# A two-block transformer on one Trainium2 core: a layer norm moved into the merge loop, gate tiles emptied by another engine, bias rows stored in longer runs

## What is computed

```python
swa_bias, swa_mask = swa_bias_and_mask(positions, rel_bias)      # once: bias by distance, per head
for l in range(DEPTH):                                           # DEPTH = 2
    h = rms_norm(x, g_mix[l])
    q_a, k_a, v_a, u_b, cq_c, ckv_c, kpe_c, gate_logits = split(h @ w_in[l])
    y_a = swa_attention(q_a, k_a, v_a, sinks, swa_bias, swa_mask)   # window of 128
    y_b = conformer_conv(u_b, ...)        # GLU, causal depthwise conv of 31 taps, LayerNorm, swish
    y_c = mla_attention(cq_c, ckv_c, kpe_c, ...)                    # latent attention
    branches = einsum('bsnc,ncd->bsnd', stack([y_a, y_b, y_c]), w_branch[l])
    gates = sigmoid(gate_logits)                                 # 3 x 1024 columns
    x = x + einsum('bsnd,bsnd->bsd', gates, branches) @ w_out[l]
    x = x + square(relu(rms_norm(x, g_mlp[l]) @ w_up[l])) @ w_down[l]
```

## Time and profile before

| | us |
|---|---|
| median of 3 runs | 4863.44 (4861.99 to 4865.29) |
| the profiled execution, its own time | 4864.94 |
| span of its instructions | 4863.1 |

### The profile page before, as it was taken

The page is one execution under the profiler, slowest core; times in us unless marked ns, Lnnn a source line. Parts: engine busy times, 40 slices in busy tenths (PEclk is TensorE's granted clock), DMA queues, the critical chain, the costliest instruction groups (busy, mean ns, idle before and its releaser), DMA issues. The chain is left out here.

```text
span 4863.1 us, 70463 instructions
## 1 busy us (share of the span) xinstructions
PE 4100.0 (84%) x29198; PEld 3345.2 (69%) x29198; DVE 2234.5 (46%) x3547; ACT 1453.8 (30%) x2611; POOL 124.8 (3%) x97
## 2 busy tenths in 40 slices
PE   6888999988889999699948888799997656657998
PEld 5666777766667777567737777688886545545887
DVE  4575544436755443334564444433333444354434
ACT  3334432223344222324222222322223201433322
POOL 0111000001100000000000000000000000000000
PEclk8999999999989999879969999899998766777999
DMA  4331444423314443100100000121121001001322
GB/s 155 89 93 50 132 156 157 160 75 95 79 56 152 156 158 137 44 14 1 61 4 3 4 3 22 38 67 61 61 68 47 6 0 35 18 0 61 96 95 78
DMA packets 320251, 338.93 MB, mean 70 GB/s; under 512 B 25792, under 2 KB 298848, under 8 KB 313696
## 3 DMA queue, kind: packets, MB, share of 16 engines
q1 hardware_dynamic: 315520, 330.56, 21.2%
q10 hardware_dynamic: 4448, 4.36, 0.3%
HBM read 313.92 MB, written 20.97 MB: 69 GB/s over the span
## 5 line engine op out<-in xcount | busy, mean ns | idle before, releaser
L276 DVE TENSOR_TENSOR weights_lo<-weight_ring,weights_hi 128x1024 fp32r<-128x1024 f32 x370 | 453.4, 1225 | 1410.0 <-ACT weights_hi L272 1410.0
L272 ACT ACTIVATE weights_hi<-weight_ring 128x1024 fp32r<-128x1024 f32 x370 | 392.2, 1060 | 1633.0 <-PE banks L323 1554.3
L323 PE MATMUL banks<-mlp_x_lo,weights_hi 128*128 128x512 f32 (+1 forms) x1280 | 480.3, 375 | 0.0
L323 PE MATMUL banks<-mlp_hidden_hi,weights_hi 128*128 128x512 f32 (+1 forms) x1280 | 477.1, 373 | 0.0
L323 PE MATMUL banks<-mlp_hidden_lo,weights_hi 128*128 128x512 f32 (+1 forms) x1280 | 476.6, 372 | 0.0
L323 PE MATMUL banks<-mlp_hidden_hi,weights_lo 128*128 128x512 f32 (+1 forms) x1280 | 476.0, 372 | 0.0
L2568 PE MATMUL banks<-weight_ring 64*64 64x64 f32 x10368 | 341.2, 221 | 86.4 <-DVE weight_ring L2686 45.7
L2568 PEld LDWEIGHTS banks<-weight_ring 64*64 64x64 f32 x10368 | 320.5, 137 | 105.2 <-DVE weight_ring L2686 52.9
L323 PE MATMUL banks<-mlp_x_hi,weights_hi 128*128 128x512 f32 x768 | 308.1, 401 | 20.2 <-DVE mlp_x_lo L307 9.5
L323 PE MATMUL banks<-mlp_x_hi,weights_lo 128*128 128x512 f32 x768 | 305.4, 398 | 0.0
L323 PEld LDWEIGHTS banks<-mlp_hidden_hi,weights_hi 128*128 128x128 f32 x1280 | 240.8, 188 | 52.6 <-issue 6.7
(11 more groups left out here) (533 smaller groups left out, 7361.3 us busy)
## 6 DMA issues: line engine op xcount, KB each, us to landing
weight_ring<-in_w SPq DMA_DIRECT2D x64, 1024.0 KB, 5.5
mod_chunks<-in_mod_w SPq DMA_DIRECT2D x24, 2048.0 KB, 10.3
weight_ring<-in_w_in SPq DMA_DIRECT2D x41, 1024.0 KB, 5.2
weight_ring<-in_w_up SPq DMA_DIRECT2D x32, 1024.0 KB, 5.7
weight_ring<-in_w_down SPq DMA_DIRECT2D x32, 1024.0 KB, 5.1
weight_ring<-in_w_in SPq DMA_DIRECT2D x52, 512.0 KB, 3.8
weight_ring<-in_w_out SPq DMA_DIRECT2D x16, 1024.0 KB, 5.3
gate_logits_dram<-gates_staged SPq DMA_DIRECT2D x48, 256.0 KB, 3.5
```

The lines of the kernel that those rows point to most:

```text
L272: act.activation(self.w_hi[:, t % 2], self._raw(t), ACT.Copy).then_inc(self.w_rounded, 1)
L276: dve.tensor_tensor(self.w_lo[:, t % 2], self._raw(t), self.w_hi[:, t % 2].bitcast(F32), ALU.subtract)\
L323: mm = pe.matmul(bank, a[:, k, :], b[:, k, t0:t0 + w], start=(k == 0 and n == 0), stop=(k == KD - 1 and n == 2))
```

## The change

1. **Bias stores.** The four mask DMAs go. The table of a part now holds 16 rows of 257 elements, the 128 values between one mask value ahead and 128 behind, just as the rows lie in DRAM. One store is then 8 runs of 16,448 bytes. Such a table is twice as large, so there are 3 instead of 8: from part 3 on ACT waits, before it writes a table, for the four stores of the part that used it. POOL fills the mask values first.
2. **Gate tiles.** `evacuate` goes from ACT to DVE, where it multiplies by the norm's row straight from the bank. The POOL step and its semaphore `scaled` go. DVE's order is: evacuate tile n, then the rest of the weights of tile n+2. The seven copies of the positional keys go from group 3's place in POOL's list to the phase's beginning, where they wait only for `placed`.
3. **Norm in the merge.** The phase `conv_finish` goes. Its steps become a class `ConvNorm` whose parts are called inside the merge's loops, behind the work of units 0 to 12. The branches are merged in the order window, latent, convolution (`MERGE_ORDER`), and the first loads of the merge are issued in the merge.

```diff
-                sp.wait_ge(filled, 16 * BLOCKS)
                 for n in range(parts_out):
                     sp.wait_ge(taken, (n + 1) * chunks // parts_out)
+                    width = held * row_out if n < parts_out - 1 else (held - 1) * row_out + P + 1
                     for b in range(BLOCKS):
-                        src = bias[n][32 * b:32 * b + 8].rearrange("h (q k) -> h q k", k=P)
-                        sp.dma_start(rows_of(b, P // parts_out * n, P // parts_out), src).then_inc(stored, 16)
+                        sp.dma_start(rows_of(b, n, width), bias[n % len(bias)][32 * b:32 * b + 8, 0:width])\
+                            .then_inc(stored[n % len(bias)], 16)
...
-                pool.memset(masked[:, :], MASKED).then_inc(blank, 1)
+                for n in range(len(bias)):
+                    pool.memset(table(n)[:, :, 0:1], MASKED)
+                    pool.memset(table(n)[:, :, P + 1:], MASKED).then_inc(blank, 1)
...
-                act.wait_ge(blank, 1)
-                for b in range(BLOCKS):
-                    act.dma_start(bias_dram[b].rearrange("h q k -> q h k"), over(masked[:, :], SWA_HEADS))\
-                        .then_inc(filled, 16)
...
+                    n, at = c // 4, c % 4 * 4
+                    if at == 0 and n < len(bias):
+                        act.wait_ge(blank, n + 1)
+                    elif at == 0:
+                        act.wait_ge(stored[n % len(bias)], stores_of(n - len(bias)))
...
-    def evacuate(self, act, n):
-        act.wait_ge(self.summed, n + 1)
+    def evacuate(self, dve, n):
+        dve.wait_ge(self.summed, n + 1)
...
-        act.activation(out, self.banks[n % 2][rows, :], ACT.Copy).then_inc(self.emptied, 1)
+        dve.tensor_tensor(out, self.banks[n % 2][rows, :], self.row[rows, :], ALU.mult).then_inc(self.emptied, 1)
...
     def dve(self, dve, halves):
         for n in self.finished(halves):
+            self.evacuate(dve, n)
             self.rest(dve, n + 2)
...
+MERGE_ORDER = (0, 2, 1)
...
         def _(pe):
+            conv.averages(pe)
             for n in range(MERGE_UNITS):
...
+                if n == 5:
+                    conv.columns(pe)
+                if n == 9:
+                    conv.widen(pe)
```

More of the change, by code:

```diff
@@ L885, in _ @@
                     act.wait_ge(made, c + 1)
-                    own = chunks // parts_out
-                    act.activation(bias[c // own][:, c % own * BANK:(c % own + 1) * BANK], ps[:, c % 8, :], ACT.Copy)\
-                        .then_inc(taken, 1)
+                    n, at = c // 4, c % 4 * 4
[3 more added lines that the diff above has]
+                        act.wait_ge(stored[n % len(bias)], stores_of(n - len(bias)))
+                    act.activation(table(n)[:, at:at + 4, 1:P + 1], ps[:, c % 8, :].rearrange("p (q k) -> p q k", k=P),
+                                   ACT.Copy).then_inc(taken, 1)
                 act.wait_ge(reduced, 1)
@@ L971, in __init__ @@
         self.landed, self.stored = [sem(f"landed{s}") for s in range(2)], [sem(f"stored{s}") for s in range(3)]
-        self.rounded, self.ready, self.summed, self.emptied, self.scaled = (
-            sem(n) for n in ("rounded", "ready", "summed", "emptied", "scaled"))
+        self.rounded, self.ready, self.summed, self.emptied = (
+            sem(n) for n in ("rounded", "ready", "summed", "emptied"))
         part = 2 * KD * P
@@ L1133, in _ @@
                 closing(sp)
[L1135 to L1141, removed]
         @block.tensor
@@ L1266, in __init__ @@
         self.keys, self.gated = keys, gated
-        self.spread, self.timed, self.folded, self.placed, self.copied = (
-            kit.ph.sem(f"kpe_{s}") for s in ("spread", "timed", "folded", "placed", "copied"))
+        self.spread, self.timed, self.folded, self.placed = (
+            kit.ph.sem(f"kpe_{s}") for s in ("spread", "timed", "folded", "placed"))
     def sync(self, sp, u, adjusted):
@@ L1338, in _ @@
             pool.wait_ge(padded, 1)
-            gates.pool(pool, (0, 1))
+            beside.pool(pool)
         @block.tensor
@@ L1669, in logit @@
     def logit(self, sp, n):
-        sp.dma_start(self.slots[:, n % 3, :], self.logits[n]).then_inc(self.read[n % 3], 16)
+        sp.dma_start(self.slots[:, n % 3, :], self.logits[MERGE_ORDER[n // KD] * KD + n % KD]).then_inc(self.read[n % 3], 16)
     def __call__(self, sp):
@@ L1676, in __call__, with merge_branches @@
             self.logit(sp, n)
-def merge_branches(kit, ys, ys_hi, ys_lo, loads, merged, bent_slots, product, following):
+def merge_branches(kit, ys, ys_hi, ys_lo, loads, merged, bent_slots, product, conv, following):
     nc, ph, ps = kit.nc, kit.ph, kit.ps
@@ L1688, in merge_branches @@
         "w_rounded", "w_ready", "x_rounded", "x_cut", "x_ready", "summed", "bent", "timed", "added"))
-    xs = [(ys[s][:, k, :], ys_hi[s][:, k, :], ys_lo[s][:, k, :]) for s in range(3) for k in range(4)]
+    xs = [(ys[s][:, k, :], ys_hi[s][:, k, :], ys_lo[s][:, k, :]) for s in MERGE_ORDER for k in range(4)]
     def raw(n):
@@ L1696, in cut_in @@
         s, t = n // KD, n % KD
-        return [4 * (s + 1) + t - 1] if s < 2 and 1 <= t <= 4 else []
+        if s == 0:
+            return [4 + t - 1] if 1 <= t <= 4 else []
+        return {12: [8, 9], 13: [10, 11]}.get(n, [])
     with ph as block:
@@ L1701, in _ @@
         def _(sp):
+            loads(sp)
             sp.wait_ge(w_ready, 2)
@@ L1737, in round_x @@
             def round_x(i):
+                if i >= 8:
+                    act.wait_ge(conv.finished, i - 7)
                 act.activation(xs[i][2], xs[i][0], ACT.Copy).then_inc(x_rounded, 1)
@@ L1742, in keep_high @@
                 act.activation(xs[i][1], xs[i][0], ACT.Copy).then_inc(x_ready, 1)
-            weights(0)
             for i in range(4):
@@ L1749, in _ @@
             keep_high(3)
+            weights(0)
             weights(1)
```

180 lines of the change are left out of this document (87 added, 93 removed).

## The result

The changed kernel takes 4821.65 us in the median of four executions (4820.95 to 4823.27), the kernel before in the same session 4862.72. The ratio is 0.9914, with a 95% interval of 0.9903 to 0.9926: 41 us faster, where 74 were forecast, and 3.7 us above the upper end of the range. The profiled execution has a span of 4820.1 us, 43.0 less than before.

What follows compares the result with a forecast made beforehand. DVE's list was taken to bound much of the window attention, stores the opening, PE the merge. Bias stores -16, gate tiles -28 and norm -30 summed to -74, giving a median of 4790 us, range 4770 to 4818.

Steps and rivals of the forecast that it cites:

- a leftover of 1.5: Opening: 1.5 us of leftover stores standing in front of the next weights, to be taken off the gain of 16.6.
- 24 KB per engine and us: Opening: rate from input loads with long rows; with 8 engines a part's store takes 2.7 us, phase end 35.5.
- The bound at the slow end: Opening: at the old 82 GB/s the eight parts take 51 us and nothing is gained, 0 instead of -16.
- rival (a): Opening: stores stay slow, ACT waits for landings at 82 GB/s, opening ends where it did; 4806 us, chance 0.14.
- The share of 37.5%: Opening: old stores' mean share of 16 DMA engines, under a half, taken to show that a store uses 8 engines.
- the 14.9 us: Attention phases: PE's 6 waits for ACT's exponents, part of the possible 14.9 + 8.4 + 8.8 us; about 10 gained.
- the bound of -18: Gate tiles: fast end per layer instead of -14, if the window attention's clock, reading 0.90, stays up.
- The two waits of half a microsecond: Latent attention: two PE waits behind ACT's evacuation that the gate tiles' change removes, -1.0 us per layer.
- rival (e): Gate tiles: taps are slow for another reason than POOL, +5 instead of -10 per layer; 4820 us, chance 0.04.
- The cutting of the first branch: Merge: ACT and DVE cut the first branch's tiles in 5.2 us, to 472.4, while PE sums for the norm.
- Rival (d): Merge: it turns serial, each of the norm's 13 steps waiting for another engine; 4881 at 3.5 us a step, chance 0.03.

Runs made afterwards that it cites:

- e2: The changed kernel with the heads' table rows on every fourth partition, the same 32 stores of 8 long runs: 4783.45 us, ratio 0.9837.
- e3: The changed kernel with rows on every fourth partition and one store of 32 rows per part, 8 stores instead of 32: 4779.07 us, ratio 0.9828.
- e7: e3 with a POOL product of SBUF rows into an unread tile put back for each gate tile: 4797.3 us, ratio 0.9863.
- e8: e3 with three POOL fills for each gate tile, reading nothing from SBUF, of about the product's length: 4780.05 us, ratio 0.9828.
- e5: The kernel before with the gate tiles' change alone (DVE empties them, key copies moved): 4832.66 us, ratio 0.9937.
- e6: The kernel before with the norm of the convolution spread over the merge, nothing else: 4832.82 us, ratio 0.9938.
- e1: The changed kernel with the opening of the kernel before (mask DMAs, eight tables, stores in 512-byte runs): 4800.82 us, ratio 0.9867.
- e4: The changed kernel with the old opening (masks, 512-byte runs) and rows on every fourth partition: 4795.21 us, ratio 0.9855.
- e9: The changed kernel with the heads' table rows on every second partition, otherwise the same: 4794.59 us, ratio 0.9851.
- e10: e4 with one store of 32 rows per part, 512 runs of 512 bytes: 4788.73 us, ratio 0.9842.

## Why the prediction was wrong, point by point

**Bias stores: wrong in sign.** Forecast -16 (the prediction's own 16.6 less a leftover of 1.5 is 15), measured +23.7. The steps ahead of the stores held: first operand at 3.96 (4.3 forecast), first store at 16.9. The step that failed is the rate of a store, "24 KB per engine and us", taken from the input loads because the runs are long like theirs. With eight engines, which was right (49.6%), it was 8.9 KB, so that the 32 stores took 57 us where some 20 were priced. What the loads and the stores don't share is which rows they touch: the loads have 128 partitions, a store has 8 neighbours. e2 changed only that and got 3.27 MB through where 1.14 went. The old stores were the nearer row in this respect: the same 8 partitions, 82 GB/s. I chose by the length of the run instead.

The bound at the slow end was mis-added besides. "At the old 82 GB/s in all the eight parts take 51 us and nothing is gained" has the doubled volume in it, since the mask values now travel with each row, but not where that leads: 51 us from 16.9 on end at 68, not at 52.1. The row alone would have given a loss of 16, at the measured 73 GB/s it is 57 us and a loss of 22 before the next phase. So rival (a) was the case that came true, priced at 4806 in place of 4790 + 16 + 16 = 4822, which would have stretched the range's upper end to the result. Even so 4822 would have hit 4821.65 by luck, since the opening lost 7.7 us more than that and the other two parts gained 8.0 more. The share of 37.5% was read as "short of engines". It was a row for a rate as well: 82 GB/s out of the same 8 partitions.

The rule of the Trainium skill (DMA: Bandwidth & Descriptors, "Why a DMA increments its semaphore by 16 and not by 1") on the number of engines that a DMA uses is borne out by the share of a half, and by e3, where 32 rows keep 16 packets in flight. It was not what decided in the changed kernel: e2 has the same eight engines.

**Gate tiles: right, somewhat low.** Forecast -14 per layer, measured -16.8 and -17.5. By stage in layer 1 the window attention gave 10.3 (forecast 10), the latent preparation 1.1 (1.0), the latent attention 5.4 (3). The term that was short is the last, and the one that fitted best was right partly by luck. The forecast counted waits of PE only. In the window attention PE's idle time fell by 8.3 us (5.8 of the exponents, 1.4 of the key copy, 1.0 of the phase change); of the 14.9 us that the prediction holds possible there, 4.8 lie in the latent attention. The other 2.1 us are PE's own busy time, 120.8 us instead of 122.9 at a granted clock of 0.92 instead of 0.90. In the latent attention the idle time fell by 2.1 us (3 forecast) and the busy time by 3.3, from 96.6 to 93.3. The granted clock was at the low level (1.2 of 2.4 GHz) for 10.2 us in two stretches before and for 3.4 us in one after, 0.96 and 0.98 in the mean. Ahead of the first stretch PE idled for 4.2 us before and 3.2 after, ahead of the second for 3.4 and 2.6. I had left the clock out of the sum and kept it in the bound of -18. The two waits of half a microsecond that I gave to ACT's evacuation didn't all go: one of 0.8 us stands unchanged, released by another ACT instruction.

The reason given for the slow taps, POOL's product on the shared ports, was shown by e7 and e8; rival (e) falls. Before, 53 of the 240 taps were slow, in the changed kernel none. Since 30 slow ones cost 17 us in e7, the 53 (some of them beside the key copies) would cost about 30, an estimate, which is nearly the whole gain of e5. What ACT's relief and the moved key copies add was not measured apart.

**Norm in the merge: right.** Forecast -15 per layer, measured -15.3 and -16.4. First sum to first merge matmul 6.24 us (6.6 forecast), one stall of 1.29 us in unit 15 and 0.07 in the next (1.6 forecast in units 15 and 16), from the very instructions that were named, and ACT's wait for `finished` of 1.55 us ends as it begins (524.79 us). The cutting of the first branch, which the prediction puts at 5.2 us from rows that give 5.6 (487.9 to 493.5), did not decide the start. The clock is 1.00 through the merge. e6 alone gives 30.5 us, the forecast was 30. Rival (d), the serial merge, has nothing in the trace: PE waits twice.

**Sum.** By the profiled executions the changed kernel took 4821.9 us where 4790.9 was forecast. The 31.0 us between them are 39.7 of the opening, less 6.3 of the gates, 1.7 of the merge and 0.7 of all else. The median less the start of the first projection matmul lies between 4733.8 and 4738.3 us for the changed kernel and the six versions of its opening (e1 to e4, e9, e10), so what lies behind the opening moves by no more than 4.5 us with it. The best kernel of these runs is e3: the changed kernel with every fourth partition and one store for each part, 86 us faster than before and 43 faster than the change.

## What to carry to other kernels

Before a DMA out of SBUF is made "larger", count the partitions that its rows lie on: a store from a few neighbouring ones runs at their rate, whatever the length of its runs, and rows spread four apart, as many as possible in one DMA, cost nothing to have here: the same instructions write them. Price a new transfer by the trace's row with the same partitions on the SBUF side, and multiply by the new volume from the time at which it starts. And a second engine's help is not free if it reads SBUF while DVE works with two operands from there: look at the slowest instances of an instruction, not only at its median.

## What the runs showed of the hardware that was not expected

- Packets of 16,448 bytes out of SBUF take 2.05 us in the median with the rows of eight engines on neighbouring partitions, 0.89 on every second, 0.61 on every fourth. When the eight start together it is 2.49, 1.26 and 0.61 us: 26 to 27 bytes/ns for four neighbouring partitions, whatever the number of rows that share them.
- Eight engines can all be busy (49.6% of 16) and move less (71 GB/s) than eight at 37.5% (82 GB/s) or at 48.4% (205 GB/s, e2). The busy share of the DMA engines includes their waiting for the partitions' way out.
- POOL suffers from the meeting as well. The seven positional key copies took 1058 ns each in the group beside the taps, and 622 in the changed kernel, where they start at 227.1 us and DVE is idle.
